# A second on-chip place for GpSimd's sum jobs, with half the scratch for its descriptors

## The chip, the cores and the metric

The kernel runs on one core of one Trainium2 chip. The metric is the device time of one execution in microseconds (us). The kernel before took 1790.06 us (median of three runs, 1789.72 to 1790.73).

## The reference

The model is cut to one layer (depth 1), so of its four mixers only the first runs, on 2048 tokens of width 1024, in float32:

```python
x = x + mixer_chunked_sgu(rmsnorm(x, norm_mix_g), w_in, v_g, w_s, b_s, w_out)
a = relu(rmsnorm(x, norm_mlp_g) @ w1)          # 1024 -> 4096
x = x + (a * a) @ w2                           # 4096 -> 1024
out = rmsnorm(x, final_g)
```

The mixer is `z = gelu(h @ w_in)`, split into `u` and `v`; `v` is normalised and mixed along 128-token chunks with lower-triangular weights; the result is `(u * s) @ w_out`.

## The kernel before, in words

TensorE does every large product in three passes (high part by high part, high by low, low by high), so every operand is loaded raw, then ScalarE writes its high part (`w_hi`, `u_hi`, `d_hi`, `x_hi`, `a_hi`) and VectorE the rest (`w_lo`, `u_lo`, `d_lo`, `x_lo`, `a_lo`). The products by `w_out`, `mlp_w1` and `mlp_w2` are made by a Strassen scheme: of a 2 by 2 split of both operands, seven products instead of eight, four of which need sums of quarters (`S1` to `S4` of the left operand, `T1` to `T4` of the weights).

**The sum jobs.** The sums of the weights, and those of the rows that go into the first MLP product, are made by GpSimd (POOL) from DRAM to DRAM, in 44 jobs (list `jobs`, L294; 4 for `w_out`, 16 for `w1`, 8 for `x`, 16 for `w2`). A job (`add_up`, L498) loads four quarters of 128x512 each, 1 MB in all, into the one tile `job`, does four dependent TENSOR_TENSORs in it, and stores the tile to `wosum`, `w1sum`, `xs` or `w2sum`. Its first act is to wait until the job before has been stored (`job_stored`), since there is one tile.

**The order on POOL** is written out by hand. `next_jobs(count)` (L548) does the next `count` jobs. In the first half it is called twice in each of the four token blocks (L556, L563): groups of 1, 2, 1, 5, 1, 3, 0 and 5 jobs, with POOL's small `rstd` rows (`v_ms`, `x_ms`) between them. In the first MLP product, which runs over 16 chunks `u` of 7 steps each, POOL waits for the first step of chunk `u` (L571) and does a group of two in chunks 0 to 3 and 9 to 13, one job in chunks 4, 5, 14 and 15, and none in 6 to 8 (L573). Then come four accumulating DMAs into `Y` (L581), the last group of four (L583), and the load of `final_g_rows`.

**Who uses the sums.** The SyncE queue (SP) loads the operands: `load_w` (L331) for the mixer's weights, `up_weight` (L354) for `u_raw`, `down_weight` (L363) for `d_raw`. Each waits until the step four before has been done by TensorE (four places for each operand); where the operand is a sum it also waits on `job_stored` for the job's number (`sums_stored`, L296). `up_operand` (L318) does the same for `x_raw`, on SP for the first half of the tokens and on ScalarE's queue for the second half. A step of the first MLP product is 24 matmuls, one of the second 48 (L1451). ScalarE splits `u_raw` in `split_u` (L608), VectorE in `split_u` (L922); VectorE also does the squares and sums of the activations between the two products (`finish_second`, L1161), in the same queue.

Of the kernel before, what the change touches and what calls it, by code (L numbers as in the profile page):

```python
# [7 lines left out]
F32 = mybir.dt.float32  # L8
# [3 lines left out]
P = 128  # L12
N = 512
# [18 lines left out]
def build(nc: bass.Bass, x, xT, gains_T, final_g, a_w_in, a_w_s, a_b_s, a_w_out,  # L32
          mlp_w1, mlp_w2, out):
    _, L, D = x.shape
# [4 lines left out]
    KU = 4  # L39
    BLOCKS = L // N  # L40
    PAIRS = BLOCKS // 2
    CHUNKS = F // (2 * N)
    EDGE = N // 2
# [21 lines left out]
    w2_v = mlp_w2.rearrange("a (c h k p) f -> c p (a h) k f", p=P, k=KU, h=2)  # L65

    w_out_q = a_w_out.rearrange("a (h k p) f -> p (a h) k f", p=P, k=KU, h=2)
    wosum = nc.dram_tensor("wosum", [P, 4, KU * N], F32, kind="Internal").ap()
    w1sum = nc.dram_tensor("w1sum", [2 * CHUNKS, P, 4, KU * EDGE], F32, kind="Internal").ap()
    w2sum = nc.dram_tensor("w2sum", [CHUNKS, P, 4, KU * N], F32, kind="Internal").ap()  # L70
    xs = nc.dram_tensor("xs", [PAIRS, P, 8, KU * N], F32, kind="Internal").ap()
# [7 lines left out]
    def region(nbytes):  # L79
        start = at[0]  # L80
        at[0] += nbytes
        return start

    def sb(name, shape, dt, offset):
        return nc.alloc_sbuf_tensor_at(name, shape, dt, offset=offset)
# [52 lines left out]
    d_hi = [sb(f"d_hi{s}", [P, KU, N], F32R, d_at[s] + UNIT) for s in range(SLOTS)]  # L138
    Y = [[sb(f"Y{b}{h}", [P, TT, D], F32, ((R, x_at[6]), (V0, V1))[b][h]) for h in range(2)] for b in range(PAIRS)]

    job = sb("job", [P, 4, N], F32, region(4 * N * 4))
    final_g_rows = sb("final_g_rows", [P, D], F32, at[0] - 4 * N * 4)
    ident = sb("ident", [P, P], F32, region(4 * P))
    gains = sb("gains", [P, 3, KD], F32, region(4 * 3 * KD))
# [19 lines left out]
    with ExitStack() as ctx:  # L164
# [3 lines left out]
        def sem(name):  # L168
            return ctx.enter_context(nc.semaphore(name))
# [38 lines left out]
        x1_ms_done, x1_rstd_done = sem("x1_ms_done"), sem("x1_rstd_done")  # L208
        x1n_ready, x1T_copied, x1T_stored = sem("x1n_ready"), sem("x1T_copied"), sem("x1T_stored")

        job_loaded, job_step, job_stored = sem("job_loaded"), sem("job_step"), sem("job_stored")

        act_read, dve_read = sem("act_read"), sem("dve_read")
        first_half, second_half = sem("first_half"), sem("second_half")
# [14 lines left out]
        def done(w, j=3):  # L229

            return 4 * w + j + 1
# [61 lines left out]
        wo_jobs = [("wo", 0, k) for k in range(KU)]  # L293
        jobs = wo_jobs + w1_jobs[:8] + s_jobs[0] + w1_jobs[8:12] + s_jobs[1] + w1_jobs[12:] + w2_jobs  # L294

        def sums_stored(kind, index):  # L296
            return 16 * (max(n for n, job in enumerate(jobs) if job[:2] == (kind, index)) + 1)

        FIRST_PARTS = ((0, 0, 1), (1, 1, 4), (0, 1, 5), (1, 0, 6))  # L300
# [17 lines left out]
        def up_operand(engine, b, i):  # L318
            op = ACT_OPERAND[i]
            if op < S2:  # L320
                engine.wait_ge(x1T_stored, 16 * 4 * (b + 1))
            else:
                engine.wait_ge(job_stored, sums_stored("x", b))
            engine.dma_start(x_raw[i][:, :, :], xs[b][:, op, :].rearrange("p (k f) -> p k f", f=N))\
                .then_inc(x_loaded[i], 16)

# [3 lines left out]
        def _(sp):  # L330
            def load_w(w):  # L331
                if w >= SLOTS:
                    sp.wait_ge(products, done(w - SLOTS))
                r = w % PER_PAIR
                if r < BOTH:
                    half = slice(r % 2 * KU, (r % 2 + 1) * KU)
                    c = (D if r % 8 < UU else 0) + r // 2 % 2 * N
                    src = w_in_v[:, half, c:c + N]
                else:
                    op = WT_OPERAND[r - BOTH]  # L340
                    if op < T2:
                        src = w_out_v[:, op // 2 * KU:(op // 2 + 1) * KU, op % 2 * N:(op % 2 + 1) * N]
                    else:
                        sp.wait_ge(job_stored, sums_stored("wo", 0))
                        src = wosum[:, op - T2, :].rearrange("p (k f) -> p k f", f=N)
                sp.dma_start(w_raw[w % SLOTS][:, :, :], src).then_inc(w_loaded[w % SLOTS], 16)

# [6 lines left out]
            def up_weight(g):  # L354
                n, op = g // STEPS % (2 * CHUNKS), WT_OPERAND[g % STEPS]
                if op < T2:
                    src = mlp_w1[n][:, op, :, :]
                else:
                    sp.wait_ge(job_stored, sums_stored("w1", n))
                    src = w1sum[n][:, op - T2, :].rearrange("p (k f) -> p k f", f=EDGE)  # L360
                sp.dma_start(u_raw[g % SLOTS][:, :, :], src).then_inc(u_loaded[g % SLOTS], 16)

            def down_weight(d):  # L363
                n, op = d // STEPS % CHUNKS, WT_OPERAND[d % STEPS]
                if op < T2:
                    src = w2_v[n][:, op // 2, :, op % 2 * N:(op % 2 + 1) * N]
                else:
                    sp.wait_ge(job_stored, sums_stored("w2", n))
                    src = w2sum[n][:, op - T2, :].rearrange("p (k f) -> p k f", f=N)
                sp.dma_start(d_raw[d % SLOTS][:, :, :], src).then_inc(d_loaded[d % SLOTS], 16)  # L370

# [53 lines left out]
            last = PAIRS - 1  # L425
            sp.wait_ge(o_ready, last * STEPS + 6)
            up_operand(sp, 0, 0)
            sp.wait_ge(products, done(out_step(last, 3)))
            up_weight(0)
# [13 lines left out]
            for g in range(SECOND):  # L443
# [3 lines left out]
                if g >= STEPS and g % STEPS in (0, 1, 2, 4):  # L447
                    part, j = {0: (0, 0), 1: (0, 1), 2: (1, 0), 4: (1, 1)}[g % STEPS]
# [31 lines left out]
        def _(pool):  # L480
# [8 lines left out]
            def rstd(sq, before, ms, ms_done, r, r_done, n, tiles=TT, plus=eps):  # L489
                for t in range(tiles):  # L490
# [4 lines left out]
                    pool.tensor_tensor(r[:, t:t + 1], ms[:, t:t + 1], minus_half[:, t:t + 1], ALU.pow)\  # L495
                        .then_inc(r_done, 1)

            def add_up(n):  # L498

                kind, index, k = jobs[n]  # L500
                if n:
                    pool.wait_ge(job_stored, 16 * n)
                if kind == "w1":
                    to = w1sum[index][:, :, k * N:(k + 1) * N]
                    pool.dma_start(job[:, :, :].rearrange("p q (k f) -> p q k f", f=EDGE),
                                   mlp_w1[index][:, :, 2 * k:2 * k + 2, :]).then_inc(job_loaded, 16)
                elif kind == "wo":
                    to = wosum[:, :, k * N:(k + 1) * N]
                    pool.dma_start(job[:, :, :].rearrange("p (h f) n -> p h (f n)", h=2), w_out_q[:, :, k, :])\
                        .then_inc(job_loaded, 16)  # L510
                elif kind == "w2":
                    to = w2sum[index][:, :, k * N:(k + 1) * N]
                    pool.dma_start(job[:, :, :].rearrange("p (h f) n -> p h (f n)", h=2), w2_v[index][:, :, k, :])\
                        .then_inc(job_loaded, 16)
                else:
                    to = xs[index][:, 4:8, k * N:(k + 1) * N]
                    pool.wait_ge(x1T_stored, 16 * 4 * (index + 1))
                    pool.dma_start(job[:, :, :], xs[index][:, 0:4, k * N:(k + 1) * N]).then_inc(job_loaded, 16)
                pool.wait_ge(job_loaded, 16 * (n + 1))
                q0, q1, q2, q3 = (job[:, i, :] for i in range(4))  # L520
                s = 4 * n
                if kind != "x":
                    pool.tensor_tensor(q3, q3, q1, ALU.subtract).then_inc(job_step, 1)  # L523
                    pool.wait_ge(job_step, s + 1)
                    pool.tensor_tensor(q1, q1, q0, ALU.subtract).then_inc(job_step, 1)
                    pool.wait_ge(job_step, s + 2)
                    pool.tensor_tensor(q0, q3, q0, ALU.add).then_inc(job_step, 1)
                    pool.wait_ge(job_step, s + 3)
                    pool.tensor_tensor(q2, q2, q0, ALU.subtract).then_inc(job_step, 1)
                else:  # L530
                    pool.tensor_tensor(q3, q2, q3, ALU.add).then_inc(job_step, 1)
                    pool.wait_ge(job_step, s + 1)
                    pool.tensor_tensor(q2, q0, q2, ALU.subtract).then_inc(job_step, 1)
                    pool.wait_ge(job_step, s + 2)
                    pool.tensor_tensor(q0, q3, q0, ALU.subtract).then_inc(job_step, 1)
                    pool.wait_ge(job_step, s + 3)
                    pool.tensor_tensor(q1, q1, q0, ALU.subtract).then_inc(job_step, 1)
                pool.wait_ge(job_step, s + 4)
                pool.dma_start(to, job[:, :, :]).then_inc(job_stored, 16)

            rstd(x_sq, x_squares(0), x_ms, x_ms_done, x_rstd, x_rstd_done, 0)
            pool.wait_ge(ws_loaded, 16)
# [3 lines left out]
            n = 0  # L546

            def next_jobs(count):  # L548
                nonlocal n
                for _ in range(count):  # L550
                    if n < len(jobs):
                        add_up(n)
                        n += 1

            for q in range(BLOCKS):
                next_jobs((1, 1, 1, 0)[q])  # L556
# [24 lines left out]
                pool.dma_start(Y[0][half][:, :, part], x1s[half][:, :, part], accum_op=ALU.add)\  # L581
                    .then_inc(x1_added[2 * half + cols], 16)
            next_jobs(len(jobs))  # L583
            pool.wait_ge(job_stored, 16 * len(jobs))
            pool.dma_start(final_g_rows[:, :], final_g.partition_broadcast(P)).then_inc(final_g_loaded, 16)
            rstd(o_sq, o_squares(0), o_ms, o_ms_done, o_rstd, o_rstd_done, 0, 2 * TT)
            for t in range(2 * TT):
# [905 lines left out]
```

## Time and profile before

| what | value |
|---|---|
| median of three runs | 1790.06 us (1789.72 to 1790.73) |
| the profiled execution | 1790.38 us; its span, first to last instruction, 1787.9 us |
| TensorE (PE) busy | 1775.5 us, 99% |
| VectorE (DVE) / ScalarE (ACT) / GpSimd (POOL) busy | 1141.8 / 786.4 / 462.9 us |
| mean granted TensorE clock | 0.999 |
| DMA queue of POOL (q0) | 27344 packets, 101.19 MB, 16.0% of the 16 engines |

The execution's own time is 2.5 us longer than its span; what lies outside the span is not shown by the trace. A busy PE means that matmuls are in flight; the share says nothing by itself about which wait ends last at a given place.

### The profile page before, as it was taken

The numbers are of one execution on the slowest core, as the hardware profiler recorded it, in microseconds if no ns is written. First come the engines' busy times: TensorE is split into PE (matmuls) and PEld (weight loads), VectorE is DVE, ScalarE is ACT, GpSimd is POOL, SyncE is SP. The second block draws the span as 40 slices with busy tenths as digits, with TensorE's granted clock in tenths as the row PEclk, the third lists the DMA queues.
The fourth block names the chain that finished last, engine by engine and source line by source line (L and its number), as shares of the span: only waits on it lengthen the run. The fifth ranks groups of instructions, "written<-read, shape, count | busy, mean of one in ns | idle before, by whom it ended". The sixth has DMA issues, their size and how long they took to land.

```text
span 1787.9 us, 20071 instructions
## 1 busy us (share of the span) xinstructions
PE 1775.5 (99%) x8036; PEld 1475.2 (83%) x8036; DVE 1141.8 (64%) x1136; ACT 786.4 (44%) x862; POOL 462.9 (26%) x418
## 2 busy tenths in 40 slices
PE   9999999999999999999999999999999999999998
PEld 7888888888888888888788888888888888888886
DVE  3564994474886655664765665575766666866665
ACT  5925235535246544434644334454433335333332
POOL 2444442242334333330013333320242002000002
PEclk9999999999999999999999999999999999999999
DMA  9555668653679888887878888999877455755552
GB/s 362 226 193 176 253 225 298 230 178 118 242 251 366 288 298 283 278 265 240 306 254 276 276 283 293 328 396 340 298 266 277 188 189 212 261 194 199 204 198 97
DMA packets 135452, 451.68 MB, mean 253 GB/s; under 512 B 8128, under 2 KB 9152, under 8 KB 119616
## 3 DMA queue, kind: packets, MB, share of 16 engines
q1 hardware_dynamic: 101344, 323.77, 51.1%
q0 software_dynamic: 27344, 101.19, 16.0%
q10 hardware_dynamic: 6672, 25.44, 3.8%
q8 instruction: 63, 1.03, 0.2%
q14 instruction: 29, 0.24, 0.0%
HBM read 320.35 MB, written 130.02 MB: 252 GB/s over the span
## 4 chain that ended last, share of the span: by engine, by line
PE 97%; DVE 1%; ACT 1%; DMA 1%; issue 0%; ACTq 0%; DVEq 0%; POOLq 0%; POOL 0%
PE bank L1451 67%; PE bank L1261 14%; PE bank L1412 9%; PE bank L1250 5%; PE bank L1314 1%; PE bank L1283 1%; DMA hT_raw<-in_xT 1%; PE bank L1317 0%; DVE Y L1188 0%; ACT x_hi L620 0%; DVE Y L1159 0%; ACT hT_hi L698 0%; DVE w_lo L919 0%; DVE x_lo L936 0%; ACT w_hi L605 0%
## 5 line engine op out<-in xcount | busy, mean ns | idle before, releaser
L1451 PE MATMUL bank<-x_hi,u_hi 128*128 128x512 f32 x896 | 349.1, 390 | 1.6 <-DVE c L1159 1.6
L1451 PE MATMUL bank<-x_hi,u_lo 128*128 128x512 f32 x896 | 348.6, 389 | 0.0
L1451 PE MATMUL bank<-x_lo,u_hi 128*128 128x512 f32 x896 | 348.6, 389 | 0.0
L1451 PE MATMUL bank<-d_hi,a_hi 128*128 128x512 f32 x896 | 348.5, 389 | 0.0
L1451 PE MATMUL bank<-d_lo,a_hi 128*128 128x512 f32 x896 | 348.5, 389 | 0.0
L1451 PE MATMUL bank<-d_hi,a_lo 128*128 128x512 f32 x896 | 348.5, 389 | 0.0
L925 DVE TENSOR_TENSOR u_lo<-u_raw,u_hi 128x1024 fp32r<-128x1024 f32 x112 | 148.5, 1326 | 169.6 <-ACT u_hi L610 169.5
L1159 DVE TENSOR_TENSOR Y<-bank,Y 128x512 f32<-128x512 f32 x208 | 137.5, 686 | 174.1 <-PE bank L1451 174.0
L615 ACT ACTIVATE d_hi<-d_raw 128x2048 fp32r<-128x2048 f32 x56 | 107.5, 1919 | 296.9 <-DMA d_raw<-w2sum 162.0
L919 DVE TENSOR_TENSOR w_lo<-w_raw,w_hi 128x2048 fp32r<-128x2048 f32 x45 | 107.9, 2402 | 146.8 <-ACT w_hi L605 146.8
L1451 PEld LDWEIGHTS bank<-x_hi,u_hi 128*128 128x128 f32 x896 | 168.2, 188 | 36.9 <-DVE u_lo L925 2.3
L1451 PEld LDWEIGHTS bank<-d_lo,a_hi 128*128 128x128 f32 x896 | 168.2, 188 | 34.9
L1451 PEld LDWEIGHTS bank<-x_hi,u_lo 128*128 128x128 f32 x896 | 168.2, 188 | 34.9
L1451 PEld LDWEIGHTS bank<-d_hi,a_hi 128*128 128x128 f32 x896 | 168.2, 188 | 34.9
L1451 PEld LDWEIGHTS bank<-d_hi,a_lo 128*128 128x128 f32 x896 | 168.2, 188 | 34.9
L1451 PEld LDWEIGHTS bank<-x_lo,u_hi 128*128 128x128 f32 x896 | 168.2, 188 | 34.8
L610 ACT ACTIVATE u_hi<-u_raw 128x1024 fp32r<-128x1024 f32 x112 | 118.2, 1057 | 165.2 <-DMA u_raw<-in_mlp_w 105.3
L931 DVE TENSOR_TENSOR d_lo<-d_raw,d_hi 128x2048 fp32r<-128x2048 f32 x56 | 131.9, 2355 | 23.1 <-ACT d_hi L615 23.1
L523 POOL TENSOR_TENSOR job<-job 128x512 f32<-128x512 f32 x36 | 64.4, 1788 | 294.0 <-DMA job<-in_mlp_w 268.3
L942 DVE TENSOR_TENSOR a_lo<-a_raw,a_hi 128x2048 fp32r<-128x2048 f32 x56 | 131.9, 2354 | 8.6 <-ACT a_hi L624 8.6
L624 ACT ACTIVATE a_hi<-a_raw 128x2048 fp32r<-128x2048 f32 x56 | 107.4, 1918 | 55.8 <-DMA a_raw<-a2s 55.8
L842 ACT ACTIVATE c<-bank 128x512 f32<-128x512 f32 x96 | 56.9, 597 | 148.8 <-PE bank L1451 137.7
(125 smaller groups left out, 2793.3 us busy)
## 6 DMA issues: line engine op xcount, KB each, us to landing
a_raw<-a2s SPq DMA_DIRECT2D x56, 1024.0 KB, 7.4
a2s<-sums SPq DMA_DIRECT2D x32, 1280.0 KB, 9.5
job<-in_mlp_w POOLq DMA_DIRECT2D x32, 1024.0 KB, 9.3
u_raw<-w1sum SPq DMA_DIRECT2D x64, 512.0 KB, 5.1
d_raw<-w2sum SPq DMA_DIRECT2D x32, 1024.0 KB, 4.9
w_raw<-in_a_w_in SPq DMA_DIRECT2D x31, 1024.0 KB, 5.8
u_raw<-in_mlp_w SPq DMA_DIRECT2D x48, 512.0 KB, 5.4
d_raw<-in_mlp_w SPq DMA_DIRECT2D x24, 1024.0 KB, 5.1
```

The source lines that it names most:

```text
L610: act.activation(u_hi[g % SLOTS][:, :, :], u_raw[g % SLOTS][:, :, :], ACT.Copy)\
L615: act.activation(d_hi[d % SLOTS][:, :, :], d_raw[d % SLOTS][:, :, :], ACT.Copy)\
L624: act.activation(a_hi[d % SLOTS][:, :, :], a_raw[d % SLOTS][:, :, :], ACT.Copy)\
L919: dve.tensor_tensor(w_lo[s][:, :, :], w_raw[s][:, :, :], f32(w_hi[s][:, :, :]), ALU.subtract)\
L925: dve.tensor_tensor(u_lo[s][:, :, :], u_raw[s][:, :, :], f32(u_hi[s][:, :, :]), ALU.subtract)\
L931: dve.tensor_tensor(d_lo[s][:, :, :], d_raw[s][:, :, :], f32(d_hi[s][:, :, :]), ALU.subtract)\
L942: dve.tensor_tensor(a_lo[s][:, :, :], a_raw[s][:, :, :], f32(a_hi[s][:, :, :]), ALU.subtract)\
L1159: dve.tensor_tensor(rows, bank_of(g, j)[:, :], rows, ALU.add).then_inc(dve_read, 1)
L1250: ins = pe.matmul(banks[j][:, :], stationary(x_part, k, j), moving(y_part, k, j), start=False, stop=k == KU - 1 and n == 2)
L1261: ins = pe.matmul(banks[j][:, :], stationary(x_part, k, j), moving(y_part, k, j), start=first and k == 0 and n == 0, stop=final and k == K ...
L1412: ins = pe.matmul(out_bank(p, i)[j][:, :], stationary[x_part][:, k, j * P:(j + 1) * P], moving[y_part][:, k, :], start=i in (0, 1, 3) and ...
L1451: ins = pe.matmul(bank_of(g, j)[:, :], stationary[x_part][:, k, j * P:(j + 1) * P], moving[y_part][:, k, :], start=i in (0, 1, 3) and k == ...
```

## The change

There are two tiles `job0` and `job1`, with a semaphore each for loading and storing; job `n` uses tile `n % 2`. `load_job(n)` waits for the store of job `n - 2` and issues the load; `add_up(n)` waits for the load, adds and stores. Within a group, `next_jobs` issues the load of job `n + 1` before job `n` is added up; across groups it does not. A user of the sums waits on both store semaphores (`wait_sums`).
```diff
-    job = sb("job", [P, 4, N], F32, region(4 * N * 4))
+    job = [sb(f"job{s}", [P, 4, N], F32, region(4 * N * 4)) for s in range(2)]
...
-        def sums_stored(kind, index):
-            return 16 * (max(n for n, job in enumerate(jobs) if job[:2] == (kind, index)) + 1)
+        def wait_sums(engine, kind, index):
+
+            n = max(n for n, j in enumerate(jobs) if j[:2] == (kind, index))
+            engine.wait_ge(job_stored[n % 2], 16 * (n // 2 + 1))
+            engine.wait_ge(job_stored[(n - 1) % 2], 16 * ((n - 1) // 2 + 1))
...
-                engine.wait_ge(job_stored, sums_stored("x", b))
+                wait_sums(engine, "x", b)
...
+            def load_job(n):
+                kind, index, k = jobs[n]
+                to = job[n % 2]
+                if n >= 2:
+                    pool.wait_ge(job_stored[n % 2], 16 * (n // 2))
...
             def add_up(n):
 
                 kind, index, k = jobs[n]
-                if n:
-                    pool.wait_ge(job_stored, 16 * n)
...
             def next_jobs(count):
+
                 nonlocal n
-                for _ in range(count):
-                    if n < len(jobs):
-                        add_up(n)
-                        n += 1
+                last = min(n + count, len(jobs))
+                if n < last:
+                    load_job(n)
+                while n < last:
+                    if n + 1 < last:
+                        load_job(n + 1)
+                    add_up(n)
+                    n += 1
...
-    nc = bacc.Bacc("TRN2", target_bir_lowering=False, num_devices=1)
+    nc = bacc.Bacc("TRN2", target_bir_lowering=False, num_devices=1, dynamic_dma_scratch_size=8192)
```

On POOL, in chunk 9 of the first MLP product (a group of two jobs, tile `job` before, `job_178` and `job_179` now), the order before is:

```order
L513 DMA job<-in_mlp_w 128x2x1024 [waits products,job_stored]
L523 TENSOR_TENSOR job<-job 128x512 [waits job_loaded]
L525 TENSOR_TENSOR job<-job 128x512 [waits job_step]
L527 TENSOR_TENSOR job<-job 128x512 [waits job_step]
L529 TENSOR_TENSOR job<-job 128x512 [waits job_step]
L539 DMA w2sum<-job 512x1x512 [waits job_step]
L513 DMA job<-in_mlp_w 128x2x1024 [waits job_stored]
L523 TENSOR_TENSOR job<-job 128x512 [waits job_loaded]
```

and now:

```order
L515 DMA job_178<-in_mlp_w 128x2x1024 [waits products,job_stored0]
L515 DMA job_179<-in_mlp_w 128x2x1024 [waits job_stored1]
L532 TENSOR_TENSOR job_178<-job_178 128x512 [waits job_loaded0]
L534 TENSOR_TENSOR job_178<-job_178 128x512 [waits job_step]
L536 TENSOR_TENSOR job_178<-job_178 128x512 [waits job_step]
L538 TENSOR_TENSOR job_178<-job_178 128x512 [waits job_step]
L548 DMA w2sum<-job_178 512x1x512 [waits job_step]
L532 TENSOR_TENSOR job_179<-job_179 128x512 [waits job_loaded1]
```

The second load has moved ahead of the first job's four additions, and between the two jobs POOL no longer waits for a store.

In the group of five in the second token block, on POOL, the second and third job now stand like this:

```order
L548 DMA w1sum<-job_178 512x1x512 [waits job_step]
L509 DMA job_178<-in_mlp_w 128x4x512 [waits job_stored0]
L532 TENSOR_TENSOR job_179<-job_179 128x512 [waits job_loaded1]
L534 TENSOR_TENSOR job_179<-job_179 128x512 [waits job_step]
L536 TENSOR_TENSOR job_179<-job_179 128x512 [waits job_step]
L538 TENSOR_TENSOR job_179<-job_179 128x512 [waits job_step]
L548 DMA w1sum<-job_179 512x1x512 [waits job_step]
L509 DMA job_179<-in_mlp_w 128x4x512 [waits job_stored1]
```

In a group of three or more, the next load thus still waits for the store that was issued just before it, ahead of additions whose operands are already there.

## Rows read from the trace of the kernel before

**Rows 1.** The page: busy time by engine, and the chain that ended last.
```profile
PE 1775.5 (99%) x8036; PEld 1475.2 (83%) x8036; DVE 1141.8 (64%) x1136; ACT 786.4 (44%) x862; POOL 462.9 (26%) x418
...
PE 97%; DVE 1%; ACT 1%; DMA 1%; issue 0%; ACTq 0%; DVEq 0%; POOLq 0%; POOL 0%
```

**Rows 2.** All waits of PE: us in total, times, longest.
```profile
PE bank L1420 <- POOL ident L483: 1.6, 1, 1.6
PE bank L1451 <- DVE c L1159: 1.6, 1, 1.6
PE bank L1261 <- DVE hT_lo L948: 1.2, 1, 1.2
PE bank L1261 <- DVE w_lo L919: 0.5, 1, 0.5
```

**Rows 3.** The chain that ended last, in order of time: start, us, what.
```profile
587.08 274.75 PE bank L1451 x1212
...
882.42 889.91 PE bank L1451 x3924
```

**Rows 4.** Stretches: length, busy us (instructions) of PE, PEld, DVE, ACT, POOL; PEclk, DMA share, GB/s.
```profile
800.00:850.00 50.00, 50.00 (x222) 41.42 (x221) 26.30 (x34) 20.31 (x29) 0.00 (x0) 1.00 0.73 242
...
1150.00:1200.00 50.00, 50.00 (x222) 41.44 (x221) 38.39 (x30) 25.12 (x27) 18.48 (x12) 1.00 1.03 402
```

**Rows 5.** Waits of POOL: us in total, times, longest.
```profile
POOL job L523 <- DMA job<-in_mlp_w: 268.3, 32, 20.1
...
POOL v_ms L492 <- ACT junk L653: 89.3, 16, 28.5
```

**Rows 6.** POOL in order of time, chunk 9: start, us, instruction, idle before.
```profile
910.76 0.71 POOL L513 DMA_DIRECT2D job<-in_mlp_w  x1 [121.05 <-PE bank L1451]
919.88 1.27 POOL L523 TENSOR_TENSOR job<-job 128x512 f32<-128x512 f32 x1 [8.40 <-DMA job<-in_mlp_w]
...
934.61 0.71 POOL L513 DMA_DIRECT2D job<-in_mlp_w  x1 [6.78 <-DMA w2sum<-job]
...
958.20 0.71 POOL L513 DMA_DIRECT2D job<-in_mlp_w  x1 [5.46 <-DMA w2sum<-job]
```

**Rows 7.** POOL in order of time: two DMAs issued one behind the other.
```profile
1252.32 1.18 POOL L581 DMA_DIRECT2D Y<-x1s  x1 [13.54 <-ACT Y L842]
1253.07 1.17 POOL L513 DMA_DIRECT2D job<-in_mlp_w  x1
```

**Rows 8.** POOL in order of time: what follows the last job's store.
```profile
1372.32 0.56 POOL L585 DMA_DIRECT2D final_g_rows<-in_final_g  x1 [5.63 <-DMA w2sum<-job]
```

**Rows 9.** SP in order of time: the first load of the last group's sums.
```profile
1388.82 0.32 SPq L370 DMA_DIRECT2D d_raw<-w2sum  x1
```

**Rows 10.** SP in order of time, chunk 9: three loads, the outer two of sums.
```profile
910.11 0.32 SPq L361 DMA_DIRECT2D u_raw<-w1sum  x1
...
915.54 0.33 SPq L361 DMA_DIRECT2D u_raw<-in_mlp_w  x1
...
920.99 0.32 SPq L361 DMA_DIRECT2D u_raw<-w1sum  x1
```

**Rows 11.** ACT in order of time, chunk 9.
```profile
921.49 1.05 ACT L610 ACTIVATE u_hi<-u_raw 128x1024 fp32r<-128x1024 f32 x1
```

**Rows 12.** DVE in order of time, chunk 9.
```profile
923.34 2.30 DVE L925 TENSOR_TENSOR u_lo<-u_raw,u_hi 128x1024 fp32r<-128x1024 f32 x1
928.01 1.23 DVE L925 TENSOR_TENSOR u_lo<-u_raw,u_hi 128x1024 fp32r<-128x1024 f32 x1 [2.37 <-ACT u_hi L610]
```

**Rows 13.** Landings of tile u_raw: from 800 to 905 us, then from 1040 to 1165 us.
```profile
DMA to landing us min/median/max: 3.4/4.7/13.3
...
DMA to landing us min/median/max: 4.0/5.2/8.7
```

**Rows 14.** DMA issues, 800 to 905 us: operation, count, KB each, median us to landing.
```profile
x_raw<-xs ACTq DMA_DIRECT2D x7, 1024.0 KB, 8.3
```

More of the change, by code:

```diff
@@ L209, in build @@
         x1n_ready, x1T_copied, x1T_stored = sem("x1n_ready"), sem("x1T_copied"), sem("x1T_stored")
-        job_loaded, job_step, job_stored = sem("job_loaded"), sem("job_step"), sem("job_stored")
+        job_step = sem("job_step")
+        job_loaded = [sem(f"job_loaded{s}") for s in range(2)]
+        job_stored = [sem(f"job_stored{s}") for s in range(2)]
         act_read, dve_read = sem("act_read"), sem("dve_read")
@@ L343, in load_w @@
                     else:
-                        sp.wait_ge(job_stored, sums_stored("wo", 0))
+                        wait_sums(sp, "wo", 0)
                         src = wosum[:, op - T2, :].rearrange("p (k f) -> p k f", f=N)
@@ L358, in up_weight @@
                 else:
-                    sp.wait_ge(job_stored, sums_stored("w1", n))
+                    wait_sums(sp, "w1", n)
                     src = w1sum[n][:, op - T2, :].rearrange("p (k f) -> p k f", f=EDGE)
@@ L367, in down_weight @@
                 else:
-                    sp.wait_ge(job_stored, sums_stored("w2", n))
+                    wait_sums(sp, "w2", n)
                     src = w2sum[n][:, op - T2, :].rearrange("p (k f) -> p k f", f=N)
@@ L496, in rstd @@
                         .then_inc(r_done, 1)
+            def load_job(n):
[3 more added lines that the diff above has]
+                    pool.wait_ge(job_stored[n % 2], 16 * (n // 2))
+                if kind == "w1":
+                    pool.dma_start(to[:, :, :].rearrange("p q (k f) -> p q k f", f=EDGE),
+                                   mlp_w1[index][:, :, 2 * k:2 * k + 2, :]).then_inc(job_loaded[n % 2], 16)
+                elif kind == "wo":
+                    pool.dma_start(to[:, :, :].rearrange("p (h f) n -> p h (f n)", h=2), w_out_q[:, :, k, :])\
+                        .then_inc(job_loaded[n % 2], 16)
+                elif kind == "w2":
+                    pool.dma_start(to[:, :, :].rearrange("p (h f) n -> p h (f n)", h=2), w2_v[index][:, :, k, :])\
+                        .then_inc(job_loaded[n % 2], 16)
+                else:
+                    pool.wait_ge(x1T_stored, 16 * 4 * (index + 1))
+                    pool.dma_start(to[:, :, :], xs[index][:, 0:4, k * N:(k + 1) * N]).then_inc(job_loaded[n % 2], 16)
@@ L498, in add_up @@
             def add_up(n):
                 kind, index, k = jobs[n]
-                if n:
-                    pool.wait_ge(job_stored, 16 * n)
[L503 to L518, printed above, removed]
@@ L519, in add_up @@
-                pool.wait_ge(job_loaded, 16 * (n + 1))
-                q0, q1, q2, q3 = (job[:, i, :] for i in range(4))
+                to = {"w1": w1sum[index % (2 * CHUNKS)][:, :, k * N % (KU * EDGE):k * N % (KU * EDGE) + N],
+                      "w2": w2sum[index % CHUNKS][:, :, k * N:(k + 1) * N],
+                      "wo": wosum[:, :, k * N:(k + 1) * N],
+                      "x": xs[index % PAIRS][:, 4:8, k * N:(k + 1) * N]}[kind]
+                pool.wait_ge(job_loaded[n % 2], 16 * (n // 2 + 1))
@@ L521, in add_up @@
+                q0, q1, q2, q3 = (job[n % 2][:, i, :] for i in range(4))
                 s = 4 * n
@@ L538, in add_up @@
                 pool.wait_ge(job_step, s + 4)
-                pool.dma_start(to, job[:, :, :]).then_inc(job_stored, 16)
+                pool.dma_start(to, job[n % 2][:, :, :]).then_inc(job_stored[n % 2], 16)
             rstd(x_sq, x_squares(0), x_ms, x_ms_done, x_rstd, x_rstd_done, 0)
@@ L583, in _ @@
             next_jobs(len(jobs))
-            pool.wait_ge(job_stored, 16 * len(jobs))
+            for i in range(2):
+                pool.wait_ge(job_stored[i], 16 * (len(jobs) // 2))
             pool.dma_start(final_g_rows[:, :], final_g.partition_broadcast(P)).then_inc(final_g_loaded, 16)
```

## The prediction, made before the changed kernel ran

> **What bounds the kernel now.** I read the page first. TensorE is busy for 1775.5 of 1787.9 us, so all its idle time is 12.4 us, and the chain that ended last lies on PE for 97% and on POOL for 0% [rows 1]. A busy share alone does not name a bound, so the list of PE's waits came next: it has four entries in the whole program, together 4.9 us, of which only the 1.6 us behind VectorE's `c` (L1159) lies in the MLP; the others belong to the start, the warm-up on `ident` and the first operands [rows 2]. None names a DMA or a sum job. The chain in order of time says where that one stall is: PE runs unbroken for 274.75 us from 587.08, and for 889.91 us from 882.42 [rows 3]; the stall ends at 882.42. Third, the stretches: PE starts 222 matmuls in 50 us whether POOL is idle or busy for 18.5 us, and whether the DMA share is 0.73 or 1.03 [rows 4]. So PE's pace answers neither to POOL's activity nor to DMA traffic; what remains is whether an operand comes late. The reader is to see that the change speeds up an engine that nothing waits for, and that it can matter only through what it collides with.
>
> POOL's own list shows what the change attacks: 268.3 us of waiting for the loads of 32 weight jobs, 8.4 us each [rows 5]. In chunk 9 one thing stands behind another: load issued at 910.76, additions from 919.88, the next load at 934.61 after 6.78 us of waiting for the store, the next group at 958.20 [rows 6].
>
> **The change, part by part.** The sum is made against the profiled execution's 1790.38 us, which stands 0.3 us above the median of the runs; I give the result for the median.
>
> *Loads ahead.* The groups hold 1, 2, 1, 5, 1, 3 and 5 jobs in the first half, then come nine groups of two and four single jobs in the first MLP product, and four jobs at the end: 44 jobs, of which 23 (all but the first of each group) get their load issued early. At 8.4 us each that is 193 us of POOL's waiting, and in a group of two the wait for the store between the jobs goes too. Such a group took 958.20 - 910.76 = 47.4 us; two waits for a store (6.8 and 5.5 [rows 6]) and one load (9.1 from issue to addition) go from it, which leaves 26 us, and the second load may add a microsecond. On the path: 0. POOL idles for 1787.9 - 462.9 = 1325 us [rows 1], and the sums are early already. The last group's are the tightest that I found: landed by 1372.32 [rows 8], first loaded by SP at 1388.82 [rows 9], 16.5 us later, and that group now ends sooner. POOL's `rstd` rows wait for ScalarE (89.3 us over 16 `v_ms` rows [rows 5]), so a POOL that comes to them earlier just waits longer.
>
> *The added wait.* In a group of three or more, the load of job n+2 waits for the store of job n, which was only just issued, and the additions of job n+1 are queued behind that wait: 5.5 to 6.8 us a job [rows 6]. It gives back part of the saving, in POOL alone; its users are those just named. On the path 0.
>
> *Double waits.* SP gets one more wait on each of 108 loads, ScalarE's queue on 4. The nearest rows are SP's own: a load with no wait on sums comes 5.43 us after one with it, and the next with it 5.45 us later [rows 10], so a wait that is satisfied costs 0.02 us at most. Ends: 0, and 4 x 0.02 = 0.1 us on ScalarE's queue; SP follows PE with margins of microseconds (below). Taken as 0.
>
> *Half the scratch.* The trace has no instruction that waits for descriptor space. Bounds: below, nothing (no gain either, since the bytes and the DMAs stay the same); above, the second issue would block until the first load has landed, 9.1 us [rows 6]. The nearest rows are the one place where POOL issues two 1 MB DMAs in a row: 1.18 and 1.17 us instead of 0.71 [rows 6, 7]. I take that, 0.5 us, on POOL only; even the upper end just gives POOL its old time back.
>
> *DMA traffic.* Two loads now stand back to back in POOL's queue, as one stretch of up to 18 us instead of two of 9 with a gap. Who could come late? A step of the first MLP product takes 274.75/1212 x 24 = 5.44 us [rows 3]. A `u_raw` load is issued when a place comes free and is due three steps, 16.3 us, later. The load of 915.54 [rows 10] is due at 931.9; ACT reads it at 921.49 without an idle time before [rows 11], and `u_lo` is ready at 923.34 + 2.30 = 925.6 [rows 12]: a margin of 6.2 us. I chose chunk 9 because there the first job starts right on POOL's release; after it POOL fell behind (a chunk is 7 x 5.44 = 38.1 us, so chunk 10's release comes at 948.9 and its group began at 958.20). Now every group of two in chunks 9 to 13 starts on its release, so chunk 9's pattern should repeat. Beside POOL's loads `u_raw` landed after 5.2 us in the median and 8.7 at most; without them, 4.7 in the median [rows 13]. A second load behind the first should keep that level for longer, not raise it: 0. The far bound is the stretch from 800 to 905 us, where another queue loaded seven 1 MB tiles [rows 14] and one `u_raw` took 13.3 us [rows 13].
> The Trainium skill ("DMA: Bandwidth & Descriptors", section "Queues, rings and completion order") states that each DMA engine goes round-robin between the queue rows that have work. By it the second POOL load takes no more of SP's share than the first, and the sum stays 0; by the far row it would be the slower case below. The trace agrees as far as 8.7 us beside single loads goes; no run here shows two job loads in POOL's queue.
>
> *Additions back to back.* `u_lo` took 2.30 us at 923.34, while POOL's additions ran, and 1.23 at 928.01 [rows 6, 12]: 1.1 us for an addition met. Four more now follow at once, at worst 4 x 1.1 = 4.4 us. They meet the next `u_lo`, ready at 928.01 + 1.23 = 929.2 and due at 920.99 + 16.3 = 937.3 [rows 10, 12], a margin of 8.1 us: 0.
> The Trainium skill ("SBUF — State Buffer", section "Who interferes with whom") states that a VectorE instruction with two SBUF inputs and a GpSimd instruction that reads SBUF exclude each other. It speaks against this change: by it VectorE can lose the whole of each addition, 4 x 1.3 = 5.2 us, still under 8.1 alone, but not if a load is late as well; the trace agrees with 1.1 for one.
>
> Sum: 0, so **1790.1 us**.
>
> **The rivals.**
> *Slower: late loads of `u_raw`.* If two loads in POOL's queue make one of SP's as late as 13.3 us, the load that had landed in at most 5.9 us (915.54 to 921.49) comes 7.4 us later, 1.2 us past its margin of 6.2. Nine groups of two run in the first MLP product: 9 x 1.2 = 10.8 us, 1800.9 us. It decides once a landing takes over 5.9 + 6.2 = 12.1 us. For it: one load did take 13.3, and what VectorE loses to additions eats into the same margin. Against: 8.7 is the most beside POOL's loads.
> *Faster.* If operands came differently, the one stall before 882.42 could go [rows 2, 3]: 1.6 us, 1788.5, still no change that shows. POOL does nothing from 800 to 850 us [rows 4] nor on to chunk 9, before or after, so I expect it to stay. A gain over 0.2% would need 3.6 of PE's 12.4 idle us, and the rest of them lie at the start and the end, which have no job in them.
> *The change does not do what it says.* With the smaller scratch the second load could be held back until the first has landed, and POOL gains little: 1790.1 us as well.
>
> **How the numbers follow.** 0.2% is 3.6 us, about what a measurement of this kernel can tell from no change. The likeliest case, nothing on the path, gets 0.94, of which 0.08 for a second load held back; the slower case gets 0.05; a gain over 0.2%, 0.01. The range runs from 1788.5 (the one stall gone) to 1793.0 (two late groups at 1.2 us, and 0.5 us for the spread of the runs). The slower case's full price lies outside it, within the 2 in 10 left out.
>
> **What would show it.** Right: PE's waits still come to about 5 us, with no DMA and no `u_lo` of a group of two among them; POOL's wait for weight loads falls from 268.3 to about 268.3 - 17 x 8.4 = 125 us (17 of the 23 early loads are of `in_mlp_w`, five of `xs`, one of `w_out`); chunk 10's first load is issued near 949 instead of 958.20; a second load's issue takes 0.7 to 1.2 us; the load of `final_g_rows` moves from 1372.32 to about 1345; `u_raw` lands within 9 us. Wrong: new PE waits behind `u_lo` in chunks 0 to 3 or 9 to 13, or more than 4 us of new idle time anywhere.

## The result, and the profile after

The changed kernel took 1807.1 us (median of four runs, 1803.29 to 1809.9) against 1789.9 before (four runs): ratio 1.0092, 95% interval 1.0081 to 1.0104. It is 17 us slower, far outside the range. The profiled execution took 1803.29 us, the fastest of its four, with a span of 1801.4 us; the account below is of the 13.5 us by which this span is longer. Lines in `kernel.py` are now 15 higher on VectorE and TensorE (L1412 is L1427, L1451 is L1466, L1054 is L1069, L919 is L934), and 2 to 15 higher on POOL.

The page of the changed kernel, busy time and the chain by engine (for [rows 1]):
```profile
PE 1779.3 (99%) x8036; PEld 1477.8 (82%) x8036; DVE 1162.3 (65%) x1136; ACT 787.2 (44%) x862; POOL 458.0 (25%) x418
...
PE 93%; DVE 3%; DMA 1%; issue 1%; ACT 1%; ACTq 0%; DVEq 0%; POOLq 0%; POOL 0%
```
PE is busy 3.8 us longer with the same 8036 instructions, and idle for 1801.4 - 1779.3 = 22.1 us instead of 12.4. The chain, which lay on VectorE for 1%, lies there for 3%. POOL is still at 0%: the engine that causes the loss is not on the chain.

PE's waits, changed kernel, the first two of seven (for [rows 2]):
```profile
PE bank L1427 <- DVE x L1069: 8.8, 2, 5.0
PE bank L1435 <- POOL ident L488: 1.6, 1, 1.6
...
```
The seven come to 14.3 us, before to 4.9. The first is new: twice, PE waits at the `w_out` product (`out_pe`) for VectorE's addition of `x` (`add_out`). Neither is in the MLP, where the prediction looked for late operands.

The stretches with those two waits, PE alone: length, busy us (matmuls started), PEclk, DMA share, GB/s. First before, then changed:
```profile
200.00:250.00 50.00, 49.96 (x228) 1.00 0.71 262
480.00:530.00 50.00, 49.96 (x227) 1.00 0.69 248
```
```profile
200.00:250.00 50.00, 45.01 (x197) 0.93 0.65 247
480.00:530.00 50.00, 45.92 (x211) 0.97 0.72 274
```
In the first, 5 us of PE go and the granted clock falls to 0.93. DMA traffic is no higher there than before.

Now the first place in order of time (start, us, instruction, idle before). VectorE before, then changed:
```profile
214.30 2.29 DVE L1036 TENSOR_TENSOR o_raw<-uT,uT 128x2048 f32<-128x2048 f32 x1
216.50 2.29 DVE L919 TENSOR_TENSOR w_lo<-w_raw,w_hi 128x2048 fp32r<-128x2048 f32 x1
218.71 2.29 DVE L1040 TENSOR_TENSOR uT<-uT,o_raw 128x2048 f32<-128x2048 f32 x1
220.91 2.29 DVE L1018 TENSOR_TENSOR o_lo<-o_raw,o_hi 128x2048 fp32r<-128x2048 f32 x1
223.11 2.48 DVE L1054 TENSOR_TENSOR x<-bank,x 128x512 f32<-128x512 f32 x4
```
```profile
214.24 3.96 DVE L1051 TENSOR_TENSOR o_raw<-uT,uT 128x2048 f32<-128x2048 f32 x1
218.12 3.38 DVE L934 TENSOR_TENSOR w_lo<-w_raw,w_hi 128x2048 fp32r<-128x2048 f32 x1
221.43 3.38 DVE L1055 TENSOR_TENSOR uT<-uT,o_raw 128x2048 f32<-128x2048 f32 x1
224.72 3.35 DVE L1033 TENSOR_TENSOR o_lo<-o_raw,o_hi 128x2048 fp32r<-128x2048 f32 x1
228.00 2.47 DVE L1069 TENSOR_TENSOR x<-bank,x 128x512 f32<-128x512 f32 x4
```
The first of these five operations starts at the same time, the fifth 4.89 us later; the four ahead of it grew by 1.67, 1.09, 1.09 and 1.06 us. What POOL does meanwhile, before and changed:
```profile
214.01 0.74 POOL L539 DMA_DIRECT2D w1sum<-job  x1 [0.30 <-POOL job L529]
226.62 0.78 POOL L505 DMA_DIRECT2D job<-in_mlp_w  x1 [11.86 <-DMA w1sum<-job]
```
```profile
213.95 0.76 POOL L548 DMA_DIRECT2D w1sum<-job  x1 [0.30 <-POOL job L538]
214.66 1.38 POOL L532 TENSOR_TENSOR job<-job 128x512 f32<-128x512 f32 x1
216.12 3.24 POOL L534 TENSOR_TENSOR job<-job 128x512 f32<-128x512 f32 x1
219.43 3.23 POOL L536 TENSOR_TENSOR job<-job 128x512 f32<-128x512 f32 x1
222.73 3.19 POOL L538 TENSOR_TENSOR job<-job 128x512 f32<-128x512 f32 x1
```
Before, POOL waited 11.86 us for a store just while VectorE ran these operations. Now the last job of the group of five (job 8, counted from 0) is loaded already and its additions run there. It has not even the added wait in front of it, since no job follows in its group.

PE at that place, before and changed:
```profile
223.51 0.39 PE L1412 MATMUL bank<-w_hi,o_lo 128*128 128x512 f32 x1
223.94 0.47 PE L1412 MATMUL bank<-w_hi,o_hi 128*128 128x512 f32 x1
```
```profile
223.44 0.39 PE L1427 MATMUL bank<-w_hi,o_lo 128*128 128x512 f32 x1
228.82 0.77 PE L1427 MATMUL bank<-w_hi,o_hi 128*128 128x512 f32 x1 [4.99 <-DVE x L1069]
229.38 0.63 PE L1427 MATMUL bank<-w_lo,o_hi 128*128 128x512 f32 x1
229.81 0.63 PE L1427 MATMUL bank<-w_hi,o_lo 128*128 128x512 f32 x1
```
Two things are to be read here. Before, matmuls started 0.23 us apart, but this one 0.43 us after the last: PE already waited 0.2 us for `x`, too short for the list of waits. The margin was nothing, and it is the same in block 3 (matmuls at 497.47 and 497.90 us). And after the stall matmuls start 0.43 us apart (229.38, 229.81) instead of 0.23: the granted clock of the stretch 228.8 to 234.0 us is 0.50, the lower level, 1.2 GHz:
```profile
228.80:234.00 5.20, 5.18 (x12) 0.50 0.60 241
```

Counting PE's matmuls one by one against those of before, the delay grows from 0 to 4.9 us at 228.82, to 7.3 by 234.0 (the lower clock), by 3.8 at the same place of block 3 (509.93 against 497.90) and 1.6 behind that. Two small delays (at 386.65 in block 2, and at 494.94) add 1.1, and PE makes up 0.6 where the kernel before waited a little too. At the last stall of the MLP the delay is 895.58 - 882.42 = 13.2 us, and the end is 13.5 us later.

### The profile page after: what moved, and what is told of

Its sections match the earlier page's. It is cut to its first block, busy times and chain, and to the rows that moved or that the text cites. A ratio compares the mean times of both kernels' runs of the same rounds, so it can differ in the third digit from the quotient of the medians.

```text
span 1801.4 us, 20076 instructions
## 1 busy us (share of the span) xinstructions
PE 1779.3 (99%) x8036; PEld 1477.8 (82%) x8036; DVE 1162.3 (65%) x1136; ACT 787.2 (44%) x862; POOL 458.0 (25%) x418
## 4 chain that ended last, share of the span: by engine, by line
PE 93%; DVE 3%; DMA 1%; issue 1%; ACT 1%; ACTq 0%; DVEq 0%; POOLq 0%; POOL 0%
PE bank L1466 65%; PE bank L1276 14%; PE bank L1427 6%; PE bank L1265 5%; PE bank L1329 1%; PE bank L1298 1%; DMA u_raw<-in_mlp_w 1%; DMA hT_raw<-in_xT 1%; DVE o_lo L1033 1%; DVE uT L1055 0%; DVE w_lo L934 0%; DVE biased L1002 0%; PE bank L1332 0%; DVE Y L1203 0%; DVE uT L1046 0%
## 5 line engine op out<-in xcount | busy, mean ns | idle before, releaser
L1466 PE MATMUL bank<-x_hi,u_hi 128*128 128x512 f32 x896 | 349.1, 390 | 1.3 <-DVE c L1174 1.3
L1466 PE MATMUL bank<-x_hi,u_lo 128*128 128x512 f32 x896 | 348.6, 389 | 0.0
L1466 PE MATMUL bank<-x_lo,u_hi 128*128 128x512 f32 x896 | 348.6, 389 | 0.0
L1466 PE MATMUL bank<-d_hi,a_hi 128*128 128x512 f32 x896 | 348.5, 389 | 0.0
L1466 PE MATMUL bank<-d_lo,a_hi 128*128 128x512 f32 x896 | 348.5, 389 | 0.0
L1466 PE MATMUL bank<-d_hi,a_lo 128*128 128x512 f32 x896 | 348.5, 389 | 0.0
L940 DVE TENSOR_TENSOR u_lo<-u_raw,u_hi 128x1024 fp32r<-128x1024 f32 x112 | 157.4, 1406 | 144.5 <-ACT u_hi L625 144.4
L934 DVE TENSOR_TENSOR w_lo<-w_raw,w_hi 128x2048 fp32r<-128x2048 f32 x45 | 108.3, 2411 | 144.0 <-ACT w_hi L620 144.0
L1466 PEld LDWEIGHTS bank<-x_hi,u_hi 128*128 128x128 f32 x896 | 168.2, 188 | 37.0 <-DVE u_lo L940 2.0
L1466 PEld LDWEIGHTS bank<-x_hi,u_lo 128*128 128x128 f32 x896 | 168.2, 188 | 35.0
L1466 PEld LDWEIGHTS bank<-d_hi,a_hi 128*128 128x128 f32 x896 | 168.2, 188 | 34.9
L1466 PEld LDWEIGHTS bank<-d_lo,a_hi 128*128 128x128 f32 x896 | 168.2, 188 | 34.9
L1466 PEld LDWEIGHTS bank<-d_hi,a_lo 128*128 128x128 f32 x896 | 168.2, 188 | 34.9
L1466 PEld LDWEIGHTS bank<-x_lo,u_hi 128*128 128x128 f32 x896 | 168.2, 188 | 34.5
L857 ACT ACTIVATE c<-bank 128x512 f32<-128x512 f32 x96 | 56.8, 597 | 142.9 <-PE bank L1466 127.4
L1174 DVE TENSOR_TENSOR c<-bank,c 128x512 f32<-128x512 f32 x96 | 65.3, 688 | 63.9 <-PE bank L1466 63.8
```

Of the source, the lines that this page charges most:

```text
L934: dve.tensor_tensor(w_lo[s][:, :, :], w_raw[s][:, :, :], f32(w_hi[s][:, :, :]), ALU.subtract)\
L940: dve.tensor_tensor(u_lo[s][:, :, :], u_raw[s][:, :, :], f32(u_hi[s][:, :, :]), ALU.subtract)\
L1174: dve.tensor_tensor(rows, bank_of(g, j)[:, :], rows, ALU.add).then_inc(dve_read, 1)
L1466: ins = pe.matmul(bank_of(g, j)[:, :], stationary[x_part][:, k, j * P:(j + 1) * P], moving[y_part][:, k, :], start=i in (0, 1, 3) and k == ...
```

## The experiments

The theory: POOL's additions take turns with VectorE operations that read two operands in SBUF (the on-chip memory of the tiles, apart from TensorE's banks); in the groups of five loads ahead put them where VectorE has no time to spare. Rivals: the smaller scratch, the loads that come earlier, and waits or places anywhere else.

**The scratch alone** (on the kernel before):
```diff
+    nc = bacc.Bacc("TRN2", target_bir_lowering=False, num_devices=1, dynamic_dma_scratch_size=8192)
```

> The kernel before with its scratch halved and nothing else. Theory (the loss is GpSimd's additions taking turns with VectorE's operations in the two groups of five): the scratch costs nothing that PE sees, 1790 us within 1 us, and PE waits 5 us in all as before. Rival (the smaller scratch delays the DMAs that GpSimd issues): some of the 17 us shows here, 1795 us or more.

Measured 1790.15 us against 1790.13, ratio 1.0001 (0.9991 to 1.001). The scratch costs nothing.

**Loads ahead outside the groups of five, then inside them only.** `next_jobs` gets an argument `ahead`; without it a job waits for the store of the one before, as it did:
```diff
+                    if not ahead:
+                        if n:
+                            pool.wait_ge(job_stored[(n - 1) % 2], 16 * ((n - 1) // 2 + 1))
+                        load_job(n)
...
+                next_jobs((2, 5, 3, 5)[q], ahead=q % 2 == 0)
```

> The changed kernel, but in the two groups of five (blocks 1 and 3) a job is loaded only when the sums before it are stored, as before the change; all other groups load ahead. Theory: the additions of those groups spread out again, PE's wait for x (8.8 us over two) is gone, and the time is 1790 us, 1788.5 to 1791.5. Rival (loads ahead, two places or the smaller scratch cost time in the mlp_w1 part or everywhere): it stays within 4 us of 1807.

> The opposite: loads ahead in the two groups of five alone, every other group as before. Theory: the whole loss is there, 1806 us, 1803 to 1809, with PE's two waits for x of together some 9 us. Rival: 1790 to 1795 us.

Measured 1793.3 us (1.0018, 1.0009 to 1.0028) and 1801.9 us (1.0064, 1.0049 to 1.0079). The groups of five cost 11.8 us, most of the loss but under the 13 expected at least, with the two waits for `x` of 8.8 us as forecast; the rest still costs 3.2, which the theory did not expect. The profile of the first shows where, in block 2 at its group of three. VectorE there before, then with the fives as before:
```profile
362.49 2.28 DVE L919 TENSOR_TENSOR w_lo<-w_raw,w_hi 128x2048 fp32r<-128x2048 f32 x1
364.69 4.79 DVE L948 SCALAR_TENSOR_TENSOR hT_lo<-hT_raw,gains,hT_hi 128x512 fp32r<-128x512 f32 x4
369.40 0.86 DVE L987 SCALAR_TENSOR_TENSOR biased<-bank,gains,bias_rows 128x256 f32<-128x256 f32 x2
```
```profile
364.26 3.37 DVE L938 TENSOR_TENSOR w_lo<-w_raw,w_hi 128x2048 fp32r<-128x2048 f32 x1
367.55 7.54 DVE L967 SCALAR_TENSOR_TENSOR hT_lo<-hT_raw,gains,hT_hi 128x512 fp32r<-128x512 f32 x4
375.01 0.86 DVE L1006 SCALAR_TENSOR_TENSOR biased<-bank,gains,bias_rows 128x256 f32<-128x256 f32 x2
```
It is the same mechanism at a third place: the additions of two jobs (11 and 12) back to back, `biased` 5.6 us later, and PE waits there twice, the second time with no releaser that the profile shows:
```profile
378.28 0.39 PE L1333 MATMUL bank<-wsT,vn_hi 128*128 128x256 f32 x1 [1.51 <-DVE biased L1012]
381.92 0.47 PE L1280 MATMUL bank<-w_hi,hT_hi 128*128 128x512 f32 x1 [1.59 <-issue]
```
Behind the second, PE runs at a granted clock of 0.58 in the mean for 4.1 us and loses 1.6 us more.

**Two jobs' additions cut** to one column of 512:
```diff
+                cols = slice(0, 1 if n in (8, 17) else N)
+                q0, q1, q2, q3 = (job[n % 2][:, i, cols] for i in range(4))
```

> The changed kernel with the four additions of jobs 8 and 17 (the last of each group of five) done on one column of 512 only, so 511 columns of these sums are left out; loads, stores, issues and counts stay. Theory (the additions meet VectorE's operations): those eight additions no longer hold VectorE up, PE's two waits for x go, 1790 us, 1788.5 to 1792. Rival (the loads that come earlier collide with others, or the stores do): nothing of that is changed, 1803 us or more.

Measured 1797.9 us (1.0041, 1.0027 to 1.0055; the seven runs lie between 1791.9 and 1800.9): half of the forecast gain. The stretch 200 to 250 us is healed, with 228 matmuls as before. In block 3 a wait for `x` of 2.8 us stays, because job 16's additions, loaded ahead too, meet three of the four operations there by themselves; and block 2's place costs 5.0 us in the profiled run, the slowest of the seven. The cut additions tell how the two engines meet. POOL and VectorE from 216 us on:
```profile
216.36 2.13 POOL L535 TENSOR_TENSOR job<-job 128x1 f32<-128x1 f32 x1
218.57 2.12 POOL L537 TENSOR_TENSOR job<-job 128x1 f32<-128x1 f32 x1
...
505.19 0.19 POOL L537 TENSOR_TENSOR job<-job 128x1 f32<-128x1 f32 x1
```
```profile
216.15 2.29 DVE L935 TENSOR_TENSOR w_lo<-w_raw,w_hi 128x2048 fp32r<-128x2048 f32 x1
218.35 2.28 DVE L1056 TENSOR_TENSOR uT<-uT,o_raw 128x2048 f32<-128x2048 f32 x1
```
An addition of one column lasts 0.19 us when it meets none of these operations, and 2.12 beside an operation of 2.28, which it does not lengthen: it waits its turn.

**The changed kernel again, and six jobs' additions cut to one column** (the same edit with `n in (8, 10, 11, 12, 16, 17)`), on one chip:

> The changed kernel once more, so that the next three are read beside it on one chip: 1803 to 1810 us, with two waits of PE for x of 9 us together (and, where the group of three in block 2 falls as in the run with the fives as before, 3 us more there).

> The changed kernel with the additions of jobs 8, 10, 11, 12, 16 and 17 done on one column of 512, so the rest of these sums is left out; every load stays ahead and every store and issue stays. Theory (additions that come back to back meet VectorE's operations in three places, the two groups of five and the group of three in block 2): PE waits for x and for biased no more, 1790 us, 1788.5 to 1792. Rival (loads ahead, the second place or the scratch cost time of their own, beside the additions): 1793 us or more.

Measured 1803.5 us (1.008, 1.0062 to 1.0099) and 1789.8 us (0.9999, 0.999 to 1.0008). The changed kernel's time falls in the range expected, but its waits for `x` come to 6.3 us, not 9.
```profile
PE bank L1427 <- DVE x L1069: 6.3, 2, 3.8
```
At the first place PE waits only 2.5 us, though the four operations together take 4.3 us longer than before. VectorE comes to them at 212.51 us instead of 214.24, because the operations in front (L1015) take 1.28 us instead of 3.10: the addition beside them waits this time (2.44 us). In the kernel before they took 3.08, beside two additions; so there, too, POOL's additions cost VectorE 1.8 us at this place, which would have been margin. Block 2 costs 3.4 us in this profile.

With every load ahead, both places and the small scratch, but with the additions of six jobs cut to one column, the loss is gone. The loads by themselves cost nothing.

**Two versions that keep all sums.** Loads ahead in the chunks and at the end only:
```diff
+                next_jobs((2, 5, 3, 5)[q], ahead=False)
```

> Loads ahead in the chunks of the mlp_w1 part and in the jobs at the end only; in all groups of the four blocks a job is loaded when the sums before it are stored. Theory: 1789.5 us, 1788.5 to 1790.5, the same as before or up to 1 us less, because the stall of 1.6 us near 881 us shrinks. Rival (part of the loss lies in the chunks of two, where u_lo meets back-to-back additions): 1793 us or more, with a wait of PE for u_lo.

Loads ahead everywhere, four jobs' additions held back:
```diff
+                if n in (8, 16, 17):
+                    pool.wait_ge(x1_attn, out_added(n // 16, 2))
+                if n == 11:
+                    pool.wait_ge(mix_read, 2 * 3 * G)
```

> The changed kernel with all loads ahead and all sums, but the additions of jobs 8, 16 and 17 held until VectorE has done the third addition of x in that product, and those of job 11 until it has done the last gate of block 2. Theory (the place of the additions decides, not their number and not the loads): 1790 us, up to 1793 if the held ones meet another chain with little to spare. Rival (the loads): 1803 us or more.

Measured 1789.9 us (0.9999, 0.999 to 1.0008) and 1789.9 us (0.9996, 0.9987 to 1.0005), each against 1790.2. Both give everything back, and neither beats the kernel before: the small gain at the stall near 881 us didn't come (1.5 and 1.9 us there). With the additions held, job 8's start at 242.99 us, and those of VectorE's operations that they meet still grow to 3.37 us; only nobody waits:
```profile
244.95 3.37 DVE L1037 TENSOR_TENSOR o_lo<-uT,o_hi 128x2048 fp32r<-128x2048 f32 x1
```

**Additions that nobody uses.** No load ahead in any group, but extra work of POOL behind one job; the diff is that of four additions, behind job 7:
```diff
+                    if n == 7:
+                        for i in range(4):
...
+                            pool.tensor_tensor(job[0][:, i, :], job[0][:, i, :], job[0][:, 3 - i, :], ALU.add).then_inc(idle_step, 1)
```

> No load ahead in any group of the blocks and in the chunks (as before the change, but with two places and the small scratch), and four additions of 128x512 that nobody uses directly behind job 7, where the changed kernel has those of job 8. No load moves. Theory (the place of the additions alone makes the loss): x comes 4.9 us late once, PE waits 5 us at the first w_out product and runs some 5 us at the lower clock behind it: 7.3 us, so 1797.4 us, 1796 to 1799. Rival (additions cost only together with loads that stand beside them): 1790 us.

> The same with two such additions. Theory (1.1 us for an addition met, no margin in front of it, and the lower clock behind the stall): 2.2 to 2.8 us late, 1.6 to 2.4 us more at the lower clock, 1794 to 1795.5 us. Rival (some microseconds of margin at that place): 1790 us.

> The same with eight fills of 128x512 with zeros in place of the additions: they write the same tile and read nothing. If GpSimd and VectorE only exclude each other where both read: VectorE's four operations keep 2.29 us, 1790 us, 1789 to 1791. If a write excludes as well: each fill met costs what it lasts, and it is 1792 us or more.

Measured 1789.3, 1790.0 and 1790.2 us (0.9996, 0.9998 and 1.0): nothing. The place was wrong by one job. Without loads ahead job 7 ends at 243.8 us, so the extra work fell at 244.5, where beside the four additions two VectorE operations grew to 3.36 and 3.38 us and PE did not wait. What this trio shows is only that. It was repeated behind job 6, with `if n == 6:` and tile `job[1]`:

> The four idle additions moved from behind job 7 to behind job 6: in this order without loads ahead, job 6's are the ones that end at 213.7 us, just before VectorE's four operations of 2.29 us (the run before put them at 244.5 us, where they cost nothing). Theory (the place of the additions alone makes the loss): x comes 4.4 to 4.9 us late once, PE waits about as long and runs some 5 us at the lower clock behind it, 7 us in all: 1797 us, 1795.5 to 1799. Rival (additions cost only beside loads that come earlier): 1790 us.

> The same place with two idle additions. Theory (1.1 us for each operation met and no margin): 2.2 to 2.8 us late and 1.6 to 2.4 us more at the lower clock, 1794 to 1795.5 us. Rival (some microseconds of margin): 1790 us.

> The same place with eight fills of 128x512 with zeros, of 0.59 us each, which write and read nothing. If only reads exclude each other: VectorE's operations keep 2.29 us, 1790 us, 1789 to 1791. If writes do too: 4.7 us of fills met cost 2 us at least, 1793 us or more.

Measured 1796.9 us (1.0038, 1.0024 to 1.0052), 1793.4 us (1.0018, 1.0009 to 1.0027) and 1790.0 us (0.9998, 0.9988 to 1.0007), against 1790.1. Additions alone, with no load moved, cost 6.9 us here and nothing 30 us later. PE's wait with four additions, then VectorE with two:
```profile
PE bank L1437 <- DVE x L1079: 5.0, 1, 5.0
```
```profile
214.25 3.94 DVE L1061 TENSOR_TENSOR o_raw<-uT,uT 128x2048 f32<-128x2048 f32 x1
218.11 3.39 DVE L944 TENSOR_TENSOR w_lo<-w_raw,w_hi 128x2048 fp32r<-128x2048 f32 x1
221.42 2.28 DVE L1065 TENSOR_TENSOR uT<-uT,o_raw 128x2048 f32<-128x2048 f32 x1
```
With two additions two of the four operations grow, by 1.65 and 1.10 us, and PE waits 2.8 us for `x`; with four all four grow and PE waits 5.0. Delay in equals stall out, so there is no margin at all. With two, the profiled span is 3.8 us longer than before (2.7 by the matmul behind the stall, 1.6 more at the lower clock, less some 0.6 made up at later waits); the medians differ by 3.3, a little under the 4 expected at least. And what POOL did with the fills, beside VectorE:
```profile
213.95 4.71 POOL L575 MEMSET job<- 128x512 f32 x8
```
```profile
215.77 2.28 DVE L944 TENSOR_TENSOR w_lo<-w_raw,w_hi 128x2048 fp32r<-128x2048 f32 x1
```
Eight fills pass beside VectorE's operations, 0.59 us each, and those keep their 2.28 and 2.29 us.

## Why the prediction was wrong

**The step that failed is *Additions back to back*.** Its mechanism and its price were right: 1.1 us for an addition met, "at worst 4 x 1.1 = 4.4 us" for a job; measured, 4.89 us (1.67 on the first operation, which meets two additions). Its place was wrong. It was weighed against one margin, the 8.1 us of `u_lo` in chunk 9, and put at 0. For `u_lo` that held: none of PE's seven waits names it. But the change also brings additions together in the groups of five and three, which the text counted under *Loads ahead* and let end at POOL's `rstd` rows. There the margin was 0 before `x` (0.2 us of PE's time already lost), twice, and less than 5.6 us at `biased`. The term put at 0 is the whole loss: with such additions cut or held the kernel takes 1789.8 and 1789.9 us, where the changed kernel takes 1803.5 on the same chip.

**What hid it.** "None names a DMA or a sum job" was read off the list of PE's waits [rows 2]. That list says that nothing was late; it does not say by how little. The stretches were read at 800 and 1150 us [rows 4], where VectorE is busy for 26 and 38 of 50 us. In the stretch 200 to 250 us of the same view it is 48 of 50, and that is the row to have read:
```profile
200.00:250.00 50.00, 49.96 (x228) 41.15 (x228) 47.98 (x46) 20.09 (x11) 20.26 (x12) 1.00 0.71 262
```
Such rows find only two of the three places: from 350 to 400 us, where block 2's lies, VectorE is busy for 38.9 of 50. *The added wait* was said to hold back the additions of the next job, in POOL alone; the last job of a group has no such wait, and job 8 is one. A late operand was priced at its lateness. It costs more: 2.4 us at the lower clock behind 4.9.

**What was right.** The Trainium skill ("SBUF — State Buffer", section "Who interferes with whom") states that a VectorE instruction with two SBUF inputs and a GpSimd one that reads SBUF exclude each other, and that one that only writes does not. The trace agrees on both: 3.38 instead of 2.29 us beside additions, 2.29 beside fills. *Half the scratch* was 0 (1.0001), and so was *Double waits*: the two versions above that keep all sums have them too (0.9999 and 0.9996). The rows read for the latter could not show it, though: SP's loads stand 5.43 and 5.45 us apart [rows 10] because a step of PE takes 5.44, whatever a wait costs. *DMA traffic* was right, now with two loads of jobs back to back; `u_raw` landings from 915 to 1165 us (for [rows 13]):
```profile
DMA to landing us min/median/max: 3.8/5.2/8.5
```
The 8.7 us called the most beside POOL's loads was read from 1040 us on; from 585 to 800 us, where the first groups of two run, it was 9.9 before and is 9.2 now, so "within 9 us" fails there by a little, without a wait of PE. The slower rival, late loads of `u_raw`, did not happen; the kernel was slower by another way than the one that stood for that side. POOL's waits and rows moved as said (for [rows 5, 6, 8]):
```profile
POOL v_ms L497 <- ACT junk L668: 127.4, 16, 47.8
POOL job L532 <- DMA job<-in_mlp_w: 120.6, 15, 20.0
```
```profile
923.93 1.44 POOL L515 DMA_DIRECT2D job<-in_mlp_w  x2 [138.32 <-PE bank L1466]
...
961.62 1.44 POOL L515 DMA_DIRECT2D job<-in_mlp_w  x2 [14.29 <-PE bank L1466]
...
1347.46 0.56 POOL L600 DMA_DIRECT2D final_g_rows<-in_final_g  x1 [10.32 <-DMA w2sum<-job]
```
POOL waits longer for `v_ms` (127.4 us, before 89.3) since it gets there sooner; 120.6 us of waiting for weight loads against the 125 forecast; two issues in 1.44 us; chunk 10's first load at 961.62 - 13.2 = 948.4 on the old scale, against 949; `final_g_rows` at 1347 against 1345, but that is 1334 on the old scale, so the agreement is chance and POOL's lead was forecast 11 us too small. The other signs on POOL held, and none of them bore on the time; the one that decided was "more than 4 us of new idle time anywhere".

**What stays open.** The four runs of the changed kernel spread over 6.6 us and the profiled one is the fastest; block 2's place was nearly free in it (0.6 us) and cost 3.4 us in the second profile (1804.05 us), where the first place cost less (a wait of 2.5 us, not 5.0). These may be what varies, but the unprofiled runs cannot show it.

## What to carry to other kernels

Before an engine off the critical path is made to do its work in another place, look where the engine that it takes turns with has no time to spare: read the stretches for an engine near 100% beside PE. A short place can hide in a stretch that is not full, so compare also the end of that engine's last operation with the start of the matmul that needs it: a list of waits shows only margins that are already below zero. A wait that seems to cost an idle engine time can be what keeps it out of another's way. If work must come early, load it early and hold the work itself back to a place with margin.

## What the runs showed of the hardware

POOL's additions and VectorE's operations with two operands in SBUF took turns. Alone, the former started 1.37 us apart and the latter 2.20; together, one of each started every 3.3 us, with 3.38 us instead of 2.29 for VectorE's operation and 3.23 instead of 1.30 for the addition. VectorE's operations with a TensorE bank as one operand (`biased`, 0.86 us for two) did not grow beside additions, and fills of 0.59 us disturbed nothing.

A stall of PE of 5.0 us was followed by 5.2 us at a granted clock of 0.50 (the lower level), and one of 3.8 us by a stretch of 4.1 us at 0.58 in the mean; these cost 2.4 and 1.6 us beside the stall. Over the runs the cost does not go by the length of the stall: it was 1.6 us behind 2.8 (two idle additions), 2.8 behind 2.8 (two jobs cut, block 3) and 2.8 behind 5.0 (four idle additions). A wait of 1.9 us for `c` in the MLP was followed by 3.5 us at 0.55 in the mean in one run (eight fills behind job 6) and by no fall of the clock in another (additions held).
